# Two transformer blocks in one TensorE-bound kernel: heads' norms by fp32 matmuls with a broadcasting ones matrix, and a reordering of VectorE, ScalarE and TensorE steps

## The reference

```python
h = rmsnorm(x, g_mix)
zb, zc, zx, zq, zk, zv = split(h @ w_in)                 # six parts of 512 columns
y_c = zb * causal_dwconv3(zc * zx, conv_w, conv_b)
q = rmsnorm(zq.reshape(b, t, 8, 64), q_norm_g)           # a norm of each head, 64 wide
k = rmsnorm(zk.reshape(b, t, 8, 64), k_norm_g)
y_a = dilated_attention(q, k, v)                         # three dilations in one softmax
x = x + concat(rmsnorm(y_c), rmsnorm(y_a)) @ w_out
h = rmsnorm(x, g_ffn)
gate = causal_dwconv3(h @ w_gate, ffn_conv_w, ffn_conv_b)    # 2816 wide
x = x + (silu(gate) * (h @ w_up)) @ w_down
x = x + sigmoid(rmsnorm(x, g_ple) @ w_ple_gate) * (p @ w_ple_proj)
```

## Time and profile before

| | us |
|---|---|
| median of 3 runs | 1756.27 |
| lowest, highest | 1753.33, 1756.96 |
| the profiled execution's own time | 1753.93 |
| its span, first to last instruction | 1752.1 |
| PE busy in the span | 1728.5 (99%) |
| DVE busy | 986.7 (56%) |
| ACT busy | 681.9 (39%) |
| weight DMA (SP's queue), share of 16 engines | 24.8% |

### The profile page before, as it was taken

One profiled execution on the slowest core, in us unless ns is written; L12 is line 12 of the kernel. 1 busy time (PEld: TensorE's weight loads), 2 busy tenths in 40 slices (PEclk: granted clock), 3 DMA queues, 4 the chain that ended last, 5 costly groups with the idle time before them and its releaser, 6 DMA issues.

```text
span 1752.1 us, 23168 instructions
## 1 busy us (share of the span) xinstructions
PE 1728.5 (99%) x9496; PEld 1477.3 (84%) x9496; DVE 986.7 (56%) x1386; ACT 681.9 (39%) x962; POOL 1.9 (0%) x11
## 2 busy tenths in 40 slices
PE   8999999999999999999999999999999999999999
PEld 7788988888889988988888889888888888888787
DVE  4776852424347576853434247757577665356655
ACT  4655441323234676441313134434455322222332
POOL 0000000000000000000000000000000000000000
PEclk9999999999999999999999999999999999999999
DMA  6222322222222212222222222122122223322341
GB/s 221 97 97 97 121 97 96 97 96 96 96 97 102 73 68 73 95 74 97 97 96 96 96 96 97 73 73 85 61 85 72 96 96 120 120 96 96 120 144 73
DMA packets 28883, 169.72 MB, mean 97 GB/s; under 512 B 2880, under 2 KB 7680, under 8 KB 9728
## 3 DMA queue, kind: packets, MB, share of 16 engines
q1 hardware_dynamic: 22592, 156.44, 24.8%
q10 hardware_dynamic: 6208, 12.08, 2.0%
HBM read 166.39 MB, written 5.27 MB: 98 GB/s over the span
## 4 chain that ended last, share of the span: by engine, by line
PE 85%; DVE 7%; ACT 5%; issue 2%; DMA 1%; DVEq 0%; SPq 0%; ACTq 0%
PE ps L1781 27%; PE ps L1783 26%; PE ps L1782 26%; ACT w_hi L456 2%; DVE w_lo L974 2%; PE ps L1918 2%; PE ps L1985 1%; DMA stage<-slabs 1%; ACT y L633 1%; PE ps L1897 1%; PE ps L2141 0%; PE ps L2274 0%; DVE relu L1207 0%; DVE act_lo L974 0%; ACT act_hi L638 0%
## 5 line engine op out<-in xcount | busy, mean ns | idle before, releaser
L1781 PE MATMUL ps<-act_hi,w_lo 128*128 128x512 f32 (+1 forms) x1512 | 544.1, 360 | 7.4 <-DVE act_lo L974 4.2
L1783 PE MATMUL ps<-act_lo,w_hi 128*128 128x512 f32 (+1 forms) x1512 | 536.9, 355 | 0.0
L1782 PE MATMUL ps<-act_hi,w_hi 128*128 128x512 f32 (+1 forms) x1512 | 536.7, 355 | 0.0
L456 ACT ACTIVATE w_hi<-stage 128x2048 fp32r<-128x2048 f32 (+4 forms) x147 | 268.3, 1825 | 376.5 <-PE ps L1783 375.5
L974 DVE TENSOR_TENSOR w_lo<-stage,w_hi 128x2048 fp32r<-128x2048 f32 (+6 forms) x152 | 323.4, 2129 | 88.1 <-ACT w_hi L456 80.9
L1781 PEld LDWEIGHTS ps<-act_hi,w_lo 128*128 128x128 f32 x1512 | 284.1, 188 | 55.0 <-issue 9.1
L1783 PEld LDWEIGHTS ps<-act_lo,w_hi 128*128 128x128 f32 x1512 | 283.9, 188 | 41.6
L1782 PEld LDWEIGHTS ps<-act_hi,w_hi 128*128 128x128 f32 x1512 | 284.1, 188 | 40.8 <-issue 1.0
L1781 PE MATMUL ps<-hid_hi,w_lo 128*128 128x512 f32 (+1 forms) x608 | 215.7, 355 | 2.1 <-DVE w_lo L974 2.1
L1782 PE MATMUL ps<-hid_hi,w_hi 128*128 128x512 f32 (+1 forms) x608 | 215.2, 354 | 0.0
L1783 PE MATMUL ps<-hid_lo,w_hi 128*128 128x512 f32 (+1 forms) x608 | 215.2, 354 | 0.0
(11 more groups left out here) (303 smaller groups left out, 2158.0 us busy)
## 6 DMA issues: line engine op xcount, KB each, us to landing
stage<-slabs SPq DMA_DIRECT2D x147, 1024.0 KB, 4.8
bias_rows<-bias_line ACTq DMA_DIRECT2D x1, 3072.0 KB, 13.8
strips<-dilated ACTq DMA_DIRECT2D x2, 1024.0 KB, 4.8
y<-x_t ACTq DMA_DIRECT2D x3, 512.0 KB, 8.7
out<-y ACTq DMA_DIRECT2D x3, 512.0 KB, 2.7
strips<-bias_rows ACTq DMA_DIRECT2D x1, 1024.0 KB, 5.1
strips<-bias_rows ACTq DMA_DIRECT2D x2, 512.0 KB, 3.7
stage<-slabs SPq DMA_DIRECT2D x3, 256.0 KB, 8.5
```

The costliest lines, as they stand in the source:

```text
L456: nc.scalar.activation(w_hi[p][:, o:o + w], stage[s][:, 0:w], ACT.Copy).then_inc(cast_hi, 1)
L1781: mm(out, l_lo, r_hi, start=start, stop=False, skip_group_check=shared)
L1782: mm(out, l_hi, r_hi, start=False, stop=False, skip_group_check=shared)
L1783: return mm(out, l_hi, r_lo, start=False, stop=stop, skip_group_check=shared)
```

## The change

The edits, in the order of the program:

1. **Start**: SP waits for the fourth piece of x before it loads slab 1 and the constants.
2. **Latent attention**: DVE casts slab 4 ahead of `wide_step("mla_kv")`.
3. **Layer norms**: ACT casts slab first+2 ahead of the squares (not after `SWA_OUT`, where slab first+3 was ahead already); DVE casts it ahead of the sum of squares; in the second half `add_half(1, 3)` goes ahead of `half_sums(1, 2)`.
4. **Sliding window, pairs 5 and 6**: the output tile's step k = 4 goes from pair 5 to between the two turns of pair 6; steps 2 and 3 move back one place each.
5. **Heads' norms**: `head_sums` is two fp32 matmuls of 512 columns with the 64x64 blocks of 1/64, `head_spread` is gone; roots and corrections by `wide_roots` and `wide_step`, on 128x1024 values; casts and convolution outputs are placed anew.
6. **Dilated heads, first half**: the fifth convolution tile has 2 steps ahead of head 2's turns and 6 behind; ACT does `turn_hi` ahead of its casts.
7. **Gated FFN**: a slab's 8 gate products come first and signal `gate_done`; DVE makes the taps from then on, multiplies silu by rstd, and only then waits for the up products; ACT's cast goes behind its `gated`.

```diff
+            sp.wait_ge(x_landed[3], 16)
             sp.dma_start(stage[1][:, :], slabs[1]).then_inc(landed[1], 16)
...
-                if first == SWA_OUT:
-                    cast(first + 3)
+                cast(first + 3 if first == SWA_OUT else first + 2)
                 act.wait_ge(slab_read, first + 1)
                 nc.scalar.activation(tmp[:, 0, :, :], y[:, 0:2, :], ACT.Square).then_inc(sq_done, 1)
-                if first != SWA_OUT:
-                    cast(first + 2)
...
-                if half and p:
-                    root("k1", 16)
-                    cast(g + p + 2)
-                else:
-                    cast(g + p + 2)
-                    root("qk"[p] + str(half), 16)
+                cast(g + p + 2)
                 if half and p == 0:
                     conv_hi(1)
+                wide_roots("qk"[p] + str(half), tmp[:, 1, :, :], qk_factor, ps[:, 4 + 2 * p:6 + 2 * p, :], 1.0)
...
                 dil_head(u)
+                turn_hi(dil, d_pt_hi, u)
                 if u == 0:
                     cast(CONV_B + 2)
                 elif u == 2:
                     cast(DIL_B)
-                turn_hi(dil, d_pt_hi, u)
...
-                        if b:
-                            cast(first + b + 2)
-                        gated(b, 0, slice(b, b + 1))
+                        gated(b, 0, slice(b, b + 1))
+                        if b:
+                            cast(first + b + 2)
...
                     for b in range(2):
+                        gated(b, i * 2, bass.ds(i * 2 + b, 1))
                         cast(first + b + 2, i * 2, SLAB)
-                        gated(b, i * 2, bass.ds(i * 2 + b, 1))
...
+                link(nc.vector.tensor_tensor(sum1[:, :], y[:, 0, :], y[:, 1, :], ALU.add))
+                cast(first + 3 if first == SWA_OUT else first + 2)
+                dve.wait_ge(sq_done, 7 * n + 1)
+                link(nc.vector.tensor_tensor(sum2[:, :], tmp[:, 0, 0, :], tmp[:, 0, 1, :], ALU.add))
...
+                add_half(1, 3)
                 half_sums(1, 2)
-                add_half(1, 3)
                 half_sums(1, 3)
                 cast(first + 6)
...
             rope_cosine(0)
+            cast(4)
             link(wide_step("mla_kv", tmp[:, 0, 1, :], sum2[:, :], ps[:, 0, :], D / KV_RANK))
...
+            def qk_factors(half, p):
                 b = 4 + 2 * p
-                dve.wait_ge(spread_done, NORM["qk"[p] + str(half)])
-                nc.vector.scalar_tensor_tensor(raw, raw, col(gain), ps[:, b:b + 2, :], ALU.mult, ALU.mult)\
-                    .then_inc(qk_full, 1)
+                link(wide_step("qk"[p] + str(half), qk_factor, tmp[:, 1, :, :], ps[:, b:b + 2, :], 1.0))
...
             cast(DIL_A + 2)
-            mean_squares("q0", 4, 1.0, 16)
-            invert_root("q0", 16)
+            qk_factors(0, 0)
             qk_full_out(0, 0)
+            qk_out(0, 1)
             qk_lo(0, 0)
-            qk_out(0, 1)
...
+            dve.wait_ge(rstd_ready, RSTD["conv"])
+            conv_scale(0)
             dve.wait_ge(dil_ready, 3)
             qk_out(1, 0)
...
+                    dve.wait_ge(gate_done, at + 1 + more)
                     nc.vector.tensor_tensor(gate[:, b, 2:T + 2], ps[:, bank, :], rstd[:, :], ALU.mult)\
                         .then_inc(ff_step, 1)
-                    nc.vector.tensor_tensor(ffh[:, b, :], ps[:, bank + 1, :], rstd[:, :], ALU.mult)\
-                        .then_inc(slab_read, 1)
...
                     dve.wait_ge(silu_done, at + 1 + more)
-                    nc.vector.tensor_tensor(ffh[:, b, :], ffh[:, b, :], silu[:, b, :], ALU.mult)\
-                        .then_inc(ffh_done, 1)
+                    nc.vector.tensor_tensor(silu[:, b, :], silu[:, b, :], rstd[:, :], ALU.mult).then_inc(ff_step, 1)
+                    dve.wait_ge(ff_step, 4 * at + 4 + more * 4)
+                    dve.wait_ge(slab_done, first + b + 1 + more)
+                    nc.vector.tensor_tensor(ffh[:, b, :], ps[:, bank + 1, :], silu[:, b, :], ALU.mult)\
+                        .then_inc(slab_read, 1)
...
                 pe.wait_ge(qk_sq, n + 1)
                 for k in range(2):
...
+                    last = nc.tensor.matmul(ps[:, bank + k, :], ones64, tmp[:, 1, k, :], start=True, stop=True)
+                last.then_inc(wide_sum, 1)
...
-            plain(g + 1, ready=between({3: lambda: head_sums(0, 4), 6: lambda: head_spread("q0", 4)}))
-            values(g + 2, between({1: lambda: k_sums(0), 2: lambda: head_spread("k0", 6)}))
+            plain(g + 1, ready=between({3: lambda: head_sums(0, 4)}))
+            values(g + 2, between({1: lambda: k_sums(0)}))
...
+                before = 2 if u == 2 else 4
+                conv_steps(2 + u, range(before))
                 if u:
                     dil_mix(u - 1)
                 turn(dil, u, d_prob)
-                conv_steps(2 + u, range(4, 8))
+                conv_steps(2 + u, range(before, 8))
```

More of the change, by code:

```diff
@@ L53 @@
 NORM = {name: n + 1 for n, name in enumerate(
-    ("mix", "q0", "k0", "q1", "k1"))}
+    ("mix",))}
 WIDE = {name: n + 1 for n, name in enumerate(
-    ("mla_q", "mla_kv", "conv", "attn", "ffn", "ple"))}
+    ("mla_q", "mla_kv", "q0", "k0", "conv", "q1", "k1", "attn", "ffn", "ple"))}
 SUM_READY = {"mla_q": 1, "mla_kv": 2, "ln": 2, "conv": 19, "ffn": 20, "ple": 21}
@@ L913, in gated @@
                     nc.scalar.activation(silu[:, b, :], gconv[:, b, :], ACT.Silu).then_inc(silu_done, 1)
-                    act.wait_ge(ffh_done, before + b + 1 + more)
+                    act.wait_ge(slab_read, first + b + 1 + more)
                     nc.scalar.activation(h_hi[:, tile, :], ffh[:, b:b + 1, :], ACT.Copy).then_inc(ffh_hi, 1)
@@ L1059, in turn_lo, with sums @@
                           pt_hi[:, BANK * n:BANK * n + w]).then_inc(a.turn_lo, 1)
[L1061 to L1073, removed]
-                    for k, part in enumerate(parts):
-                        ins = nc.vector.tensor_tensor(dst[:, :], dst[:, :], part, ALU.add)
-                        if k < len(parts) - 1:
-                            link(ins)
-                    if last:
-                        ins.then_inc(sum_ready, 1)
-                    else:
+            def sums(squares, squared, first, last):
+                dve.wait_ge(sq_done, squared)
+                if first and len(squares) == 2:
+                    ins = nc.vector.tensor_tensor(sum2[:, :], squares[0], squares[1], ALU.add)
+                    squares = []
+                elif first:
+                    ins = nc.vector.tensor_copy(sum2[:, :], squares[0])
+                    squares = []
+                for k, part in enumerate(squares):
+                    ins = nc.vector.tensor_tensor(sum2[:, :], sum2[:, :], part, ALU.add)
+                    if k < len(squares) - 1:
                         link(ins)
+                if last:
+                    ins.then_inc(sum_ready, 1)
+                else:
+                    link(ins)
             def add(t, c, source, scaled):
@@ L1098, in layer_norm @@
                 add_out(first, 0, scaled=scaled)
-                if first == SWA_OUT:
-                    cast(first + 3)
                 dve.wait_ge(slab_read, first + 1)
-                sums([0, 1], [tmp[:, 0, k, :] for k in range(2)], 7 * n + 1, True, False, True)
+                link(nc.vector.tensor_tensor(sum1[:, :], y[:, 0, :], y[:, 1, :], ALU.add))
+                cast(first + 3 if first == SWA_OUT else first + 2)
+                dve.wait_ge(sq_done, 7 * n + 1)
+                link(nc.vector.tensor_tensor(sum2[:, :], tmp[:, 0, 0, :], tmp[:, 0, 1, :], ALU.add))
                 if first != SWA_OUT:
-                    cast(first + 2)
                     cast(first + 3)
@@ L1300, in _ @@
             c_scale(4)
-            cast(4)
             rope_sine(0)
@@ L1660, in rms_out @@
                 squares = p_raw if gain == "g_ffn" and n == 3 else tmp[:, n % 2, :, :]
-                sums(tiles, [squares[:, k, :] for k in range(len(tiles))], squared + n + 1, n == 0, last, False)
+                sums([squares[:, k, :] for k in range(len(tiles))], squared + n + 1, n == 0, last)
             n_hi = [4]
@@ L2205, in _ @@
                     pe.wait_ge(cast_lo, SWA_OUT + 1)
-                    out_steps(1, range(3))
+                    out_steps(1, range(2))
+                elif p == 6:
+                    out_steps(1, (4,))
                 elif p == 7:
@@ L2348, in _ @@
                 score(dil, u + 1, dil_operands, 0)
-                conv_steps(2 + u, range(4))
+                before = 2 if u == 2 else 4
+                conv_steps(2 + u, range(before))
                 if u:
@@ L2363, in _ @@
             pe.wait_ge(dil.turn_lo, 3 * 4)
-            plain(g + 1, ready=between({3: lambda: head_sums(2, 4), 6: lambda: head_spread("q1", 4)}))
-            values(g + 2, between({1: lambda: k_sums(1), 2: lambda: head_spread("k1", 6)}))
+            plain(g + 1, ready=between({3: lambda: head_sums(2, 4)}))
```

(14 more changed lines are left out.)

76 lines of the change are left out of this document (31 added, 45 removed).

## The result

| | before | after |
|---|---|---|
| median, us | 1756.33 | 1729.53 |
| lowest, highest, us | 1753.33, 1756.96 | 1729.16, 1731.37 |
| the profiled execution's own time, us | 1753.93 | 1731.37 |
| ratio, 95% interval | | 0.9853 (0.9836 to 0.987) |

The change takes 26.8 us off the median where 23.3 were forecast (1733.0, range 1727 to 1742). The two profiled executions are 22.6 us apart, close to the sum of the prediction (22.2). So there are two questions: whether the terms of the sum are each right, and where the further 4 us between the medians are.

A forecast was written before the change was run, and what follows sets the result against it. PE was taken to bound the kernel. Terms of 0 + 0.85 + 7.1 + 0.45 + 10.4 + 0.9 + 2.5 = 22.2 us gave 1731.7 from the profiled execution, 1734.1 from the median; forecast 1733.0 us, range 1727 to 1742.

The forecast's parts named there:

- What bounds: Whole kernel: PE is busy 1728.5 of 1752.1 us, so an edit must take work from PE or end its wait.
- Layer norms: Layer norms: reordered casts and adds end PE's waits for low parts and an add, 7.1 us, bounds 4.5 and 7.5.
- (c): Layer norms, second half: statistics come up to 0.8 us earlier, shortening waits for activations' low parts, 2.0 us.
- (a): Three layer norms: the stall of 1.21 us behind the cast of slab first+2 goes, 3.65 us.
- (b): One layer norm's second half: the wait of 1.3 us for the last add goes, 1.45 us.
- The rival, that the waits are handed on: Layer norms: removed waits return at the next sum or low part, 3 to 4 us back, 1737; chance 0.10.
- Heads' norms: Heads' norms: spreads leave PE and two fp32 matmuls replace tiny sums, 10.4 us, the largest term.
- sums and waits: Heads' norms: new sums cost 0.2 us more in all, while PE's waits of 0.7 us there go.
- The rival of the late chain: Heads' norms: chain of about 10 us makes PE wait behind `values`, 4 to 5 us back, 1738; chance 0.12.
- The clock: Behind the last tiny head sums: a half-clock stretch goes with the tiny matmuls and the wait ahead, 1.5 us.
- Gated FFN: Gated FFN: three waits worth 3.15 us go, 0.6 new at round starts, net 2.5 us, bounds 0 and 3.2.
- the rival "slower": Gated loop: one chain per slab, about 10.1 us, exceeds PE's 11.0 and bounds the kernel, 1757 or more; chance 0.03.

The follow-up runs named there:

- heads_slow: The changed kernel with ScalarE's square in each head norm's roots made five times instead of once: 1751.13 us, ratio 0.9976.
- tiny_back: The changed kernel with the 16 tiny matmul records put back ahead of each fp32 head sum: 1737.58 us.
- ffn_slow: The changed kernel with VectorE's first product of each gated slab made three times: 1754.42 us, ratio 0.9996.
- second measurement: The changed kernel run again unchanged, for its own scatter: 1729.35 us (1728.5 to 1730.96).

## Why the prediction was right, and where its sizes were off

**What bounds** was right: PE at 99% before and after, and every gain is either work taken from PE or a wait ended. Adding something to each printed wait was right, but 0.16 us was too little, since it was read from the first step alone: 1.05 printed gave 1.3 us, 0.69 printed 1.0, and 1.33 printed 1.6.

**Start**: 0 forecast, none found (ratio 1.0003 alone). **Latent attention** 0.85, found 1.0. **Sliding window** 0.45, found 0.4. **Dilated heads** 0.9, found 1.0.

**Layer norms**: 7.1, found 7.1 by the median and 8.2 in the profile. Term (c) was 2.0 and is 2.7: each of the three norms gave 0.9 us, where 0.8, 0.4 and 0.8 were counted. I also misread the row behind it: the three waits of the L974 row that aren't at the start are 0.9 us in all (4.2 less 1.3 and 1.9 at the start) and lie in the first and third norm, and the last norm's 0.7 us is in another row (act_lo L978). The other 0.4 us are 0.1 at each of the four waits of (a) and (b). The rival, that the waits are handed on, didn't occur.

**Heads' norms**: 10.4, found 12.0 in the profile and 11.6 to 13.2 by the medians. The spreads are 8.5 for 8.4, the new sums 1.73 for 1.74. The mis-sized term is "sums and waits": -0.2 + 0.7 forecast, 1.9 found. The old trains cost 1.80 us each, not 1.70, so the new sums bring 0.3 where 0.2 was taken off. I gave the three waits at these places no surcharge, against my own rule, and they bring 1.3 (0.5, 0.5 and 0.3), not 0.7. The last 0.3 is no effect of the edit that can be shown: it is the pace of half 0's `values` products, 0.118 us apart in before's trace and 0.113 in after's. The chain to `qk_full` is 6.1 us for 6.4, and PE didn't wait. The rival of the late chain had the right mechanism at the wrong place: heads_slow shows that the first thing to be late is the square ahead of k's sums, not `conv_steps(0)`.

**The clock** is the step that failed in size. I took one stretch of 1.5 us from one profile and tied it to the tiny matmuls and the wait together. The mean clocks say that before loses about 1.7 stretches in an execution and after 0.2. That is 1.5 x 1.5 = 2.3 us by the difference, where 1.5 were counted. As to the cause, in tiny_back the train alone did not bring it, and in heads_slow waits of 3.1 and 3.9 us did. But a short wait alone doesn't account for it either: the five profiles with the old layer norms have twenty waits of 1.0 to 1.3 us there, and none has a stretch behind them. So at k's sums the train and the wait together, as the prediction had it, remain the best account; the wait of 0.28 us without the train is untested. Edit 7's waits, too, were by the profiles and mean clocks worth more than their length, for which the sum had no term.

**Gated FFN**: 2.5, found 2.8 to 2.9 in the profiles and 3.8 by the median; the 0.6 at the rounds' starts was right, the three waits gave 3.4, not 3.15. Of the rival "slower", the chain was estimated at 10.1 us and is 10.26, against 11.0 estimated and 10.88 found for PE's slab, so the margin was 0.6 us, not 0.9. Its break-even was put at 1.0 us over, by 22 slabs that each pay. ffn_slow lost 24.9 us at 0.82 over, so the point lies lower, though by another sum: the slabs paid 12.9 us, and the rounds' ends, which the rival did not count, 11.4.

**The number.** 22.2 by the sum. Found on the median: 26.8, and 26.2 in the second measurement. The edits' steps add up to 25.4, 3.2 more than the sum: 1.1 in the norms, 1.4 in the heads' sums and waits, 0.3 in the FFN and 0.4 in the rest. The clock's further stretches are worth about 1 us by the mean clocks, an estimate; what is then left is within the scatter of before's own medians (1755.3 to 1756.3). The gain of the profile pair, 22.6, met the sum by luck: 3.2 us too little in the terms were hidden by 1.6 us of half clock in after's execution and 1.1 us of pace. I had also put the answer between two ways to carry the sum over to the median (1731.7 and 1734.1), which happened to err on the far side of both.

## What to carry to other kernels

On a kernel whose bounding engine is 99% busy, list that engine's waits one by one, price each from start to start, up to where the steps are normal again, rather than as printed, and ask of each edit only which of these it ends: the terms here came out within 0.4 us but for two, of 1.1 and 1.4 us. Price the substitute of a piece of work by a row of the same form in the same trace, and for a chain moved to other engines look first at what is queued behind it there, not only at who reads its end. Before a single profile is taken for the median, compare the mean clock of the other executions: a wait that brings a stretch at half clock in some of them is worth more than its length.

## What the runs showed of the hardware

The clock of TensorE went to half (1.2 GHz) for stretches of 3.4 us at the same three places in this program: behind the wait at the start (four of the five profiles in which it is 1.84 us or more, none of the nine in which it is 1.55 to 1.77), behind k's sums of half 1, with a wait of 0.28 us ahead of tiny matmuls (5 of the 6 profiles that have both), and behind a wait of 1.3 us in the FFN, with one of 0.56 us just ahead of it (3 of 5). It came in some executions and not in others of the same program. It came with waits of 3.1 and 3.9 us in heads_slow, where the clock was already down in the last microsecond of the second, and the stretch there was 6.8 us long. It did not come behind tiny matmuls without a wait (one profile), nor behind twenty waits of 1.0 to 1.3 us in the layer norms (five profiles). A stretch costs about 1.5 us and 0.001 of the mean clock, and such stretches make most of the 3 to 5 us by which executions of before differ.

A wait of TensorE cost 0.23 to 0.3 us more than its printed length, spread over two steps (1.05 printed, 1.28 lost; 0.69 printed, 1.0 lost). Two fp32 matmuls of 512 columns cost 1.73 us, 8 fp32 matmuls of 2 columns 1.80 us. Products of 256 columns started 0.113 or 0.118 us apart for whole stretches, and which of the two a stretch had differed between executions.
